# Two or three projection jobs run side by side through the eight operand steps, at three places of a three-layer block kernel

## The reference, cut to what matters

```
def odd_mixer(h, w_in, dw_w, dw_b, ln_g, ln_b, w_out):
    ...
    cn = (cf - mu) * lax.rsqrt(var + EPS) * ln_g.astype(jnp.float32) + ln_b.astype(jnp.float32)
    y = jax.nn.silu(cn).astype(h.dtype) * jax.nn.silu(gate)
    return y @ w_out
...
        x = x + rms_norm(y, post_norm[layer])
...
        xn = rms_norm_2(h, norm_mix_g[layer])
        proj = jnp.einsum('bld,de->ble', xn, w_in[layer])
```

## Time and profile before

| what | value |
|---|---|
| median of 3 runs | 2128.55 us |
| the profiled execution | 2128.05 us |
| its span, first to last instruction | 2126.0 us |
| mean granted TensorE clock | 0.984 |
| TensorE busy | 2040.2 us, 96% |
| VectorE busy | 1332.6 us, 63% |
| GpSimd busy | 1093.5 us, 51% |
| ScalarE busy | 685.5 us, 32% |

### The profile page before, as it was taken

How to read it: one execution, slowest core, us unless ns; L and a number is a source line. 1 busy time by engine, 2 the same in 40 slices (tenths; PEclk the granted TensorE clock), 3 DMA queues, 4 the chain that set the end, 5 groups by cost and what they waited for, 6 DMA issues and landing times. The chain is left out here.

```text
span 2126.0 us, 25084 instructions
## 1 busy us (share of the span) xinstructions
PE 2040.2 (96%) x9336; PEld 1602.1 (75%) x9336; DVE 1332.6 (63%) x1846; ACT 685.5 (32%) x1146; POOL 1093.5 (51%) x932
## 2 busy tenths in 40 slices
PE   7999999999999999899999899999899999999997
PEld 6887877777776767787788565677788887888886
DVE  6137553679998898442264467656644446777768
ACT  3002543331125331421021244423222223554542
POOL 3222015467684884344334200025877787888885
PEclk9999999999999999899999999999999999999998
DMA  5332017444453443346523443335556767666652
GB/s 184 139 119 79 22 41 244 177 159 139 159 197 129 168 139 99 120 174 190 170 90 106 114 96 71 105 134 163 187 193 209 233 217 277 215 246 226 217 178 108
DMA packets 103352, 331.24 MB, mean 156 GB/s; under 512 B 12544, under 2 KB 12800, under 8 KB 102464
## 3 DMA queue, kind: packets, MB, share of 16 engines
q1 hardware_dynamic: 55040, 190.64, 27.8%
q0 software_dynamic: 29808, 104.35, 14.2%
q10 hardware_dynamic: 18384, 34.66, 4.4%
HBM read 268.55 MB, written 46.20 MB: 148 GB/s over the span
## 5 line engine op out<-in xcount | busy, mean ns | idle before, releaser
L1221 PE MATMUL PS<-XHM,WH 128*128 128x512 f32 (+1 forms) x1464 | 526.5, 387 | 23.6 <-DVE XLM L2473 13.0
L1221 PE MATMUL PS<-XLM,WH 128*128 128x512 f32 (+1 forms) x1464 | 511.7, 377 | 0.0
L1221 PE MATMUL PS<-XHM,WL 128*128 128x512 f32 (+1 forms) x1464 | 509.1, 375 | 0.0
L966 POOL DMA_DIRECT2D WH<-weights x145 | 83.6, 577 | 817.7 <-PE PS L1221 800.2
L973 POOL TENSOR_TENSOR WL<-WRAW,WH 128x1024 fp32r<-128x1024 f32 x145 | 351.8, 2426 | 25.1 <-DMA WH<-weights 20.2
L1221 PEld LDWEIGHTS PS<-XHM,WH 128*128 128x128 f32 x1464 | 271.1, 190 | 94.1 <-issue 19.4
L1221 PEld LDWEIGHTS PS<-XLM,WH 128*128 128x128 f32 x1464 | 278.0, 190 | 56.0 <-issue 3.4
L1221 PEld LDWEIGHTS PS<-XHM,WL 128*128 128x128 f32 x1464 | 277.8, 190 | 52.1
L2697 DVE SCALAR_TENSOR_TENSOR PS<-G,TAPW,PS 128x512 f32<-128x512 f32 x348 | 262.7, 755 | 11.7
L3213 DVE TENSOR_TENSOR ACC<-ACC,PS 128x1024 f32<-128x1024 f32 x112 | 119.7, 1082 | 19.2 <-PE PS L1221 16.9
L1221 PE MATMUL PS<-OPH,VSH 128*128 128x512 f32 x256 | 101.0, 394 | 1.9 <-issue 1.9
(11 more groups left out here) (377 smaller groups left out, 3957.6 us busy)
## 6 DMA issues: line engine op xcount, KB each, us to landing
WRAW<-weights SPq DMA_DIRECT2D x207, 512.0 KB, 3.5
WH<-weights POOLq DMA_DIRECT2D x191, 512.0 KB, 4.6
OPR<-inner SPq DMA_DIRECT2D x56, 512.0 KB, 6.4
inner<-STAGE ACTq DMA_DIRECT2D x56, 256.0 KB, 4.9
inner<-TOUT ACTq DMA_DIRECT2D x48, 256.0 KB, 5.0
XTOK<-x SPq DMA_DIRECT2D x8, 512.0 KB, 7.1
x_kept<-X SPq DMA_DIRECT2D x4, 1024.0 KB, 7.2
X<-x_kept SPq DMA_DIRECT2D x8, 512.0 KB, 5.1
```

Of the source, the lines that this page charges most:

```text
L966: g.dma_start(WH[:, u, :], weights[WORDER[p]]).then_inc(w_hi[u], 16)
L1221: m = nc.tensor.matmul(dst[:, a:b], w, v[:, a:b], start=first and n == 0, stop=last and n == 2)
```

## The change

A new function `half_jobs` runs several jobs at once. With a lag for each job, it goes through t = 0, 1, 2, ... and at each t issues for every job the three matmuls of step k = t - lag. Only the first job waits for operands, since the others are never ahead of it. Each job waits for its weights and its bank where its own k is 0. Place 1 runs jobs 0 and 1 with lags 0 and 4, place 2 jobs 0, 1 and 2 with lags 0, 1 and 4, place 3 jobs 0 and 1 with lags 0 and 1. The other jobs of the three places run one by one as before. On GpSimd one step is moved: at p = P_OUT1B + 3 the low part of the weights of p - 1 is computed ahead of `high(p)`, which waits for the end of job P_OUT1B.

```
             for p in range(P_END):
+                if p == P_OUT1B + 3:
+                    low(p - 1)
                 high(p)
-                if p >= 1:
+                if p >= 1 and p != P_OUT1B + 3:
                     low(p - 1)
...
+            def half_jobs(p, jobs, lags, x_ready):
+
+                for t in range(KD + lags[-1]):
+                    for i, (job, lag) in enumerate(zip(jobs, lags)):
+                        k, u, h = t - lag, (p + i) % NW, job[2]
+                        if not 0 <= k < KD:
+                            continue
+                        if k == 0:
+                            pe.wait_ge(w_ready, p + i + 1)
+                            wait_freed(pe, JOBS[JOB[job] - 4])
+                        if i == 0:
+                            pe.wait_ge(x_split, x_ready + k + 1)
+                        m = three(ring(job), WH[:, u, k * P:(k + 1) * P], WL[:, u, k * P:(k + 1) * P],
+                                  XH[:, k, tokens(h)], XL[:, k, tokens(h)], k == 0, k == KD - 1, ((0, HALF),))
+                        if k == KD - 1:
+                            m.then_inc(half_full, 1)
...
-                for k in range(KD):
-                    half_job(P_OUT1A + k, (OUT1, k, 0), X_OUT1[0] if k == 0 else None)
+                half_jobs(P_OUT1A, [(OUT1, k, 0) for k in range(2)], (0, 4), X_OUT1[0])
+                for k in range(2, KD):
+                    half_job(P_OUT1A + k, (OUT1, k, 0))
...
-                for k in range(KD):
-                    half_job(P_OUT1B + k, (OUT1, k, 1), X_OUT1[1] if k == 0 else None)
+                half_jobs(P_OUT1B, [(OUT1, k, 1) for k in range(3)], (0, 1, 4), X_OUT1[1])
+                for k in range(3, KD):
+                    half_job(P_OUT1B + k, (OUT1, k, 1))
...
+                half_jobs(P_IN2B, [(IN2, c, 1) for c in range(2)], (0, 1), X_IN2[1])
                 for i, c in enumerate((*range(8), *range(17, 21))):
-                    half_job(P_IN2B + i, (IN2, c, 1), X_IN2[1] if i == 0 else None)
+                    if i >= 2:
+                        half_job(P_IN2B + i, (IN2, c, 1))
```

## The result

The median after is 2131.36 us (2130.03 to 2135.88, 12 runs), beside 2128.7 us for the kernel before (2126.79 to 2131.68, 12 runs). The ratio is 1.0015, 95% interval [1.0008, 1.0022]: 1.7 to 4.7 us slower, where 0.6 faster was forecast. The time lies inside the range and within the 0.2% called no change, but the sign was wrong and the interval excludes the forecast. The profiled execution of after takes 2134.08 us, its span is 2132.0.

What follows compares the result with a forecast made beforehand. TensorE was taken to be held by operand waits (13.0 us) at three places, with GpSimd's weight path next behind. The terms 0.9 - 1.9 + 0.4 = -0.6 took 2128.05 to 2127.5 us, range 2123.0 to 2132.5.

Steps and rivals of the forecast that it cites:

- Place 3: Pair with lags 0 and 1: 0.4 us slower, between 2.1 faster and 4.1 slower, GpSimd's late issue not recurring.
- Place 2: Three jobs side by side: 1.9 us faster, between 4.6 faster and 2.1 slower, job 3 starting 3.4 us earlier.
- Place 1: Pair with lags 0 and 4: 0.9 us slower, between 0.3 and 2.1, job 2's weights hanging on job 0's later end.
- That a shift reaches the end: Between places: a TensorE shift at place 1 passes through VectorE and back unreduced; place 2's passes to place 3 too.
- GpSimd's weight path is later than I take it: Rival, chance 0.14: late landing at place 2 and GpSimd's 3.0 us again at place 3; sum +6.4, 2134.4 us.
- The weights are in time: Rival, chance 0.12: landings near 3.7 us and the clock holds at all three places; -6.4, 2121.7 us.
- Changing jobs costs a restart: Rival, chance 0.02: some 43 changes of job on TensorE cost 0.1 us each; -0.6 + 4.3, 2131.8 us.
- What was said to show it wrong: Signs: no wait for WL at place 2 or 3, or a high on GpSimd issued long after its job ended.

Runs made afterwards that it cites:

- ring_after: The whole change plus two small DMAs (128 x 32 bytes) on GpSimd some 85 us ahead of place 3; 2126.91 us, ratio 0.9988.
- p2_only_code: Kernel before with only place 2's three jobs side by side and moved low, plus 16 transposes made twice at TensorE's start; 2131.75 us, one run.
- order1: Kernel before, jobs one by one, with GpSimd's low and next high at place 1 set ahead of the convolution sums; 2124.53 us, ratio 0.998.
- best: The change plus order1's GpSimd order, places 2 and 3 as pairs (lags 0, 3), an earlier low at place 3, two small DMAs; 2117.43 us, ratio 0.995.
- p2_hold_code: p2_hold with 16 transposes made twice at the start of TensorE's program; 2128.18 us, one run.
- p2_hold: p2_only with both loads of P_OUT1B + 4 held back until the high of P_OUT1B + 3 has landed; 2128.4 us, ratio 0.9997.
- p2_only: Kernel before with only place 2 changed: three jobs side by side and GpSimd's moved low; 2127.11 us, ratio 0.9994.
- p2_pair: Kernel before with only place 2 changed: two jobs side by side (lags 0, 3) instead of three, moved low; 2125.13 us, ratio 0.9983.

## Why the prediction was wrong, step by step

**Place 3 is the step that failed.** The sentence was that GpSimd's late issue is taken "as not recurring, since the same issue at place 2 came at once". It recurred: 2.96 us in after. The working around it held. Job 0's end was put at 967.9 and ScalarE's reaction 0.3 later; measured, 970.93 less the 2.53 that after was late there, that is 968.4. From there 0.6 and 2.4 to the start of job 2 make 971.2 as forecast, and 974.37 is measured, the pause and 0.2. The clock behind the wait was put at 1.5 and took 1.6, though the wait was 4.62 and not some 2. The term was +0.4; with the pause it is +3.4, and +3.61 came. My upper end, 4.1, had it in. With the pause out of the way, in ring_after, job 2 starts 1.21 earlier than before, where 1.15 was forecast, but behind its wait of 1.93 the clock did not fall (0.03 us lost, 1.5 priced): so this price was a guess too. The evidence was in the earlier trace rows: 13.10 of idle time with no releaser, in the kernel before. An issue of another job that came at once says nothing about a pause which sits on one issue by number.

**Place 2 was mis-sized**, -1.9 forecast and +0.20 measured. The steps up to job 0's end are right (its `high` at 885.8 forecast, 888.17 less 2.33, that is 885.84, measured; the operand waits and the half clock went as said). The landing was put at 4.6 and 0.3 more for two `high` that overlap; it took 6.2, so job 3 came 2.2 us earlier than before and not 3.4, behind a wait of 3.98 instead of 3.0, and the clock took 2.4 instead of 1.5. The overlap, which I priced at 0.3, costs 0.2 at most by p2_only_code. What I had not looked for is TensorE's own code load. It comes with TensorE's place in its program, and the interleaving brought it onto the `high`: in before it begins at 895.78, some 5 us behind the landing of that `high`. With it out of the way the place gives -1.96 and -2.07, near the forecast -1.9, with job 3 3.6 and 3.7 earlier and the clock at 1.7. What the clock takes was never fixed by the rows: ring_after's 1.4 stands behind nearly the same wait as in after.

**Place 1 was right.** Job 2 was forecast at 695.04 and came at 694.96; the wait was put at 4.1 and is 3.99. +0.9 was forecast, +0.53 measured in after: the shift of job 2 is the 0.5 of it, the 0.3 more for the clock did not come. Which size is typical one trace can't say, since the untouched place itself reads 0, -0.4 or -1.5 with the clock. Behind the same wait of 4.0 the clock took 1.2 more in ring_after, which reads +1.69, inside the 0.3 to 2.1 given.

**That a shift reaches the end** is right for the losses of after: its +2.30 at 700 us is +2.33 at place 2. It is only half right for gains at place 1. VectorE's chain at 730 us takes back what goes beyond some 3.2 us, as order1 and best show; I had looked at VectorE's wait of the earlier trace rows alone.

**The rivals.** "GpSimd's weight path is later than I take it" named the right path and both places, at a chance of 0.14. Its reason at place 2, loads that fall together, was not the cause, and its price, +6.4, was too high, because the landing took 6.2 and not 8.9. "The weights are in time" was wrong for after, and is what best brings about. "Changing jobs costs a restart" was wrong: in after's shared steps the matmuls of place 3 start 0.23 us apart (966.09, 966.32, 966.55, 966.79), as they do within one job. That the rule of the Trainium skill, page "TensorE: Matmul & The Clock Gate", section "Loop structure matters more than you think", would have the change cost by itself was my reading: the section's bad case is a wait ahead of every matmul, and it says nothing of two output tiles taken in turn. What it wants, dense matmuls, is what the change brought at place 2: 53 of them in 16.0 us, where before there were 22 in 13.6.

**What was said to show it wrong** was there: a `high` on GpSimd issued long after its job ended.

## What to carry to other kernels

Before an engine's waits for one input are filled with the next job's work, look up what that job's other input hangs on; here a slot that is freed later moves the whole weight path, and at place 1 reordering the in-order engine that prepares the weights was worth as much as the interleaving could bring. An idle time with no releaser in a trace is a cost with an unknown place, and stays in the sum until a run moves it. A transfer that gates an engine should be checked for what else falls into it after the shift, the engine's own code loads included.

## What the runs showed of the hardware that was not expected

- GpSimd stops for 2.7 us once in this program, at the DMA that carries its count (pieces by the program's shapes, and 16 for each DMA) over a number between 16,368 and 16,416. Two tiny DMAs more move the stop two jobs earlier.
- A 16 KB load of TensorE's code, 0.98 us on one of 16 transfer engines, in the middle of a 512 KB load moves that load's landing from 4.8 (p2_hold_code) to 6.0 us (p2_hold) after its issue. The Trainium skill, page "DMA: Bandwidth & Descriptors", section "Issuing engines are not separate DMA queues", says that transfers of all issuing engines interleave on the same 16 DMA engines; the trace agrees, and adds the code loads to them.
- The same unchanged code of place 1 met a fall of TensorE's clock behind the wait for WL of 1.96 us (before), ahead of that wait (six traces) or not at all (p2_only and p2_pair, with waits of 1.93 and 1.95). The place came 0, 0.4 or 1.5 us shorter by this alone. At place 2 the clock took 1.4 behind a wait of 3.81 and 3.0 behind one of 3.80 (ring_after, p2_hold). What decides it stays open.
